# First block's attention: the weights' low halves by an accumulating DMA onto negated high halves, and every rotation on VectorE

## The reference, cut to what matters

```python
n = rmsnorm(h, attn_norm[l])
proj = n @ w_in[l]                                  # u, v_sgu, q, k, v_att: 512 columns each
...
q = apply_partial_rope(q, cos, sin)                 # 4 heads of 2 x 64; 16 of each 64 are rotated
k = apply_partial_rope(k, cos, sin)
... scores, causal softmax, p[:, :, 0] - lam * p[:, :, 1], times v_att ...
h = h + mixed @ w_out[l]                            # 512 rows from the gating, 512 from the attention
h = h + conv_ffn(rmsnorm(h, ffn_norm[l]), w_up[l], conv_w[l], conv_b[l], w_down[l])

def apply_partial_rope(t, cos, sin):
    half = ROT_DIM // 2
    t1 = t[..., :half]
    t2 = t[..., half:ROT_DIM]
    rot = jnp.concatenate([t1 * cos - t2 * sin, t2 * cos + t1 * sin], axis=-1)
    return jnp.concatenate([rot.astype(t.dtype), t[..., ROT_DIM:]], axis=-1)
```

## Time and profile before

| | |
|---|---|
| time, median of 3 runs (lowest to highest) | 1814.74 us (1811.52 to 1820.94) |
| the profiled execution: its time | 1814.2 us |
| its span in the profile | 1812.5 us |
| mean granted TensorE clock | 0.994 |

### The profile page before, as it was taken

How to read it: one execution, slowest core, us unless ns; L and a number is a source line. 1 busy time by engine, 2 the same in 40 slices (tenths; PEclk the granted TensorE clock), 3 DMA queues, 4 the chain that set the end, 5 groups by cost and what they waited for, 6 DMA issues and landing times. The chain is left out here.

```text
span 1812.5 us, 26067 instructions
## 1 busy us (share of the span) xinstructions
PE 1765.2 (97%) x8977; PEld 1440.3 (79%) x8977; DVE 1122.1 (62%) x1826; ACT 780.8 (43%) x1270; POOL 1037.3 (57%) x1265
## 2 busy tenths in 40 slices
PE   8999999999999999999999999999999999999998
PEld 6876888888888886788888888877666778988886
DVE  4788656566656338766666655644476567655665
ACT  5434543333334335453333333466566663333332
POOL 6574445555465557364555554457311558888885
PEclk9999999999999999999999999999999999999999
DMA  7221224443423221133444332413201112233221
GB/s 253 94 102 50 82 82 151 150 151 115 150 93 117 93 98 54 48 105 112 144 162 148 130 115 82 140 49 118 92 1 48 47 47 94 94 117 114 96 93 47
DMA packets 103206, 184.70 MB, mean 102 GB/s; under 512 B 7322, under 2 KB 67404, under 8 KB 101068
## 3 DMA queue, kind: packets, MB, share of 16 engines
q1 hardware_dynamic: 102940, 183.44, 28.8%
q10 hardware_dynamic: 176, 0.07, 0.0%
HBM read 180.35 MB, written 2.10 MB: 101 GB/s over the span
## 5 line engine op out<-in xcount | busy, mean ns | idle before, releaser
L1003 POOL TENSOR_TENSOR w_lo<-raw,w_hi 128x256 fp32r<-128x256 f32 (+1 forms) x1124 | 911.6, 845 | 751.0 <-ACT w_hi L1089 747.5
L2499 PE MATMUL ps<-n_hi,w_hi 128*128 128x512 f32 (+1 forms) x1320 | 507.1, 384 | 3.9 <-ACT zc L1394 1.8
L2501 PE MATMUL ps<-n_hi,w_lo 128*128 128x512 f32 (+1 forms) x1320 | 501.1, 380 | 0.0
L2500 PE MATMUL ps<-n_lo,w_hi 128*128 128x512 f32 (+1 forms) x1320 | 500.7, 379 | 0.0
L1089 ACT ACTIVATE w_hi<-raw 128x1024 fp32r<-128x1024 f32 (+2 forms) x331 | 307.8, 937 | 359.6 <-PE ps L2501 240.8
L2499 PEld LDWEIGHTS ps<-n_hi,w_hi 128*128 128x128 f32 x1320 | 249.0, 189 | 53.1 <-issue 6.0
L2501 PEld LDWEIGHTS ps<-n_hi,w_lo 128*128 128x128 f32 x1320 | 249.0, 189 | 48.0
L2500 PEld LDWEIGHTS ps<-n_lo,w_hi 128*128 128x128 f32 x1320 | 249.3, 189 | 45.4 <-issue 0.2
L2043 DVE TENSOR_TENSOR ps<-ps,sq 128x512 f32<-128x512 f32 x88 | 61.3, 699 | 179.8 <-PE ps L2501 177.4
L2499 PE MATMUL ps<-x_hi,w_hi 128*128 128x512 f32 x416 | 167.0, 401 | 0.1
L2501 PE MATMUL ps<-x_hi,w_lo 128*128 128x512 f32 x416 | 162.6, 391 | 0.0
(11 more groups left out here) (359 smaller groups left out, 2668.5 us busy)
## 6 DMA issues: line engine op xcount, KB each, us to landing
raw<-in_w_up SPq DMA_DIRECT2D x44, 1024.0 KB, 6.9
raw<-in_w_ff SPq DMA_DIRECT2D x32, 1024.0 KB, 6.6
raw<-in_w_in SPq DMA_DIRECT2D x26, 1024.0 KB, 6.1
zb<-in_ada_w SPq DMA_DIRECT2D x16, 1536.0 KB, 8.3
raw<-in_w_down SPq DMA_DIRECT2D x44, 512.0 KB, 3.9
raw<-in_w_out SPq DMA_DIRECT2D x12, 1024.0 KB, 6.1
raw<-in_w_in SPq DMA_DIRECT2D x4, 512.0 KB, 8.2
za<-in_x SPq DMA_DIRECT2D x4, 512.0 KB, 6.1
```

Source lines behind the costliest of these rows:

```text
L1003: last = pool.tensor_tensor(part[0], part[1], part[2], ALU.subtract)
L2499: pe.matmul(out, l_hi, r_hi, start=start, stop=False)
L2500: pe.matmul(out, l_hi, r_lo, start=False, stop=False)
L2501: return pe.matmul(out, l_lo, r_hi, start=False, stop=stop)
```

## The change

For the 32 quarters of the kinds `Q` and `D4` (16 in each layer) the low half is made in another way. ACT writes the high half as before and then, right behind it, the negated high half into `w_lo`. POOL, in place of four subtractions, waits for that, issues accumulating DMAs that add `raw` onto `w_lo` (four of 128x2x128 for a `Q` quarter, two of 128x2x256 for a `D4` one, two rows `k` each), waits until all have landed, and tells it with a small memset. Every rotation is on VectorE: heads 1 to 3, tile by tile, in the even steps 0 to 10 (`rope_at`). The waits of `swap_rows` are now for the DVE instruction that last read the half of `swapped`, two tiles back.

```diff
+ADDED_KINDS = ("Q", "D4")
+def rope_at(n):
+
+    return (1 + n // 4, n // 2 % 2) if n % 2 == 0 and n <= 10 else None
...
                     emptied(sp, ("qk"[j], l, t))
-                    if t == 0 and l:
-                        sp.wait_ge(rope_set, 6 * l - 1 + j)
-                    elif t == 1:
-                        sp.wait_ge(swap_read, 2 * l + 1 + j)
-                    elif t:
-                        sp.wait_ge(rope_set, 6 * l + 2 * t + j - 3)
+                    if n >= 2:
+                        sp.wait_ge(swap_read, n - 1)
...
+                if g in added_at:
+                    n = added_at[g]
+                    pool.wait_ge(wneg_ready, n + 1)
+                    to, raw_ = split_quarter(st.kind, w_lo.bitcast(F32), g % 4, q), source(st, q)
+                    for k in range(0, to.shape[1], 2):
+                        pool.dma_start(to[:, k:k + 2], raw_[:, k:k + 2], accum_op=ALU.add).then_inc(wadd_in, 16)
+                        added[0] += 16
+                    pool.wait_ge(wadd_in, added[0])
+                    pool.memset(mark[:, n % 8:n % 8 + 1], 0.0).then_inc(wlo_ready, 1)
+                    return
...
-            def rope(l, t, j):
-
-                x_ = (qT, kT)[j][:, t, :]
-                n = 8 * l + 2 * t + j
-                k = 2 * (6 * l + 2 * t + j - 2)
-                turned = swapped[:, n % 2, :]
-                if t == 1 and j == 0:
-                    pool.wait_ge(qk_ready, 2 * l + 2)
-                pool.wait_ge(swap_in[n % 2], 64 * (n // 2 + 1))
-                pool.tensor_tensor(x_, x_, cosF, ALU.mult).then_inc(rope_step, 1)
-                pool.tensor_tensor(turned, turned, sinF, ALU.mult).then_inc(rope_step, 1)
-                pool.wait_ge(rope_step, k + 2)
-                pool.tensor_tensor(x_, x_, turned, ALU.add).then_inc(rope_set, 1)
...
                 act.activation(split_quarter(st.kind, w_hi, g % 4, q), source(st, q),
                                ACT.Copy).then_inc(whi_ready, 1)
+                if g in added_at:
+                    act.activation(split_quarter(st.kind, w_lo, g % 4, q), source(st, q), ACT.Copy, scale=-1.0)\
+                        .then_inc(wneg_ready, 1)
...
                     x_ = (qT, kT)[j][:, t, :]
                     n = 8 * l + 2 * t + j
+                    if n >= 2:
+                        dve.wait_ge(qk_ready, n - 1)
                     dve.wait_ge(swap_in[n % 2], 64 * (n // 2 + 1))
...
-                    dve.wait_ge(swap_read, 2 * l + j + 1)
+                    dve.wait_ge(swap_read, n + 1)
...
+                    if (turned := rope_at(n)) is not None:
+                        rope(*turned)
                     if n < 2:
                         sgu_gate(2 + n)
```

More of the change, by code:

```diff
@@ L549, in build @@
         swapped = sb("swapped", [P, 2, S])
+        mark = sb("mark", [P, 8])
         banks = ctx.enter_context(nc.psum_tensor("ps", [P, 8 * S], F32))
@@ L557, in build @@
         whi_ready, wlo_ready = sem("whi_ready"), sem("wlo_ready")
+        wneg_ready, wadd_in = sem("wneg_ready"), sem("wadd_in")
         quarter_done = sem("quarter_done")
@@ L568, in build @@
         ang_ready, rope_ready = sem("ang_ready"), sem("rope_ready")
-        swap_zero, swap_read, rope_step, rope_set = (sem("swap_zero"), sem("swap_read"), sem("rope_step"),
-                                                     sem("rope_set"))
+        swap_zero, swap_read = sem("swap_zero"), sem("swap_read")
         swap_in = [sem(f"swap_in{i}") for i in range(2)]
@@ L739, in last_added @@
             return free[4 + i % 4], BK.ffn2[4 + i % 4] + 2 * (FG2 - 1) + i // 4 + 1
+        added_at = [st.at[q] for st, q in by_quarter if st.kind in ADDED_KINDS]
+        added_at = {g: n for n, g in enumerate(added_at)}
         def landed_value(st):
@@ L980, in _ @@
             pool.memset(swapped[:, :, :], 0.0).then_inc(swap_zero, 1)
+            added = [0]
             def lo(g, value, used, pieces=range(LO_PARTS)):
@@ L1026, in gains_and_weights @@
                 lo(g + 1, g + 2, g - 2, range(2, 4))
-            def rope(l, t, j):
-                x_ = (qT, kT)[j][:, t, :]
-                n = 8 * l + 2 * t + j
-                k = 2 * (6 * l + 2 * t + j - 2)
-                turned = swapped[:, n % 2, :]
-                if t == 1 and j == 0:
-                    pool.wait_ge(qk_ready, 2 * l + 2)
-                pool.wait_ge(swap_in[n % 2], 64 * (n // 2 + 1))
-                pool.tensor_tensor(x_, x_, cosF, ALU.mult).then_inc(rope_step, 1)
-                pool.tensor_tensor(turned, turned, sinF, ALU.mult).then_inc(rope_step, 1)
-                pool.wait_ge(rope_step, k + 2)
-                pool.tensor_tensor(x_, x_, turned, ALU.add).then_inc(rope_set, 1)
-            rope_before = {STR["qk", l, 0].g0 + 7 + i: (l, 1 + i // 2, i % 2) for l in range(DEPTH) for i in range(6)}
             done = 0
@@ L2744, in _ @@
                         if i == 0:
[L2745 to L2748, removed]
+                            pe.wait_ge(qk_ready, l * 8 + 2 * hd + 2)
                         for m in range(2):
```

2 lines of the change are left out of this document (removed).

## The result

The changed kernel takes 1961.96 us (median, 1956.12 to 1963.08) against 1814.75 of the kernel before. The ratio is 1.080, with a 95% interval of 1.0765 to 1.0836: slower by 147 us, far outside the predicted range.

What follows compares the result with a forecast made beforehand. PE, busy 97% of the span, was taken as the bound. Layer 0 +10.8, layer 1 -4.1, `D4` quarters +0.2 and DVE +1.4 made +8.3 us on 1814.2, 1822.5, hence 1823 against the median; range 1807 to 1852.

Steps and rivals of the forecast that it cites:

- What bounds: Whole kernel: PE is busy 97% of the span; the change could give back at most 13.5 us.
- which chain is hit: Layer 0, low half 15 to step 0's scores: scores may start at 98.7 + 3D, 118.8 against 108.60, +10.2 us.
- D: Time from a `Q` quarter's negated half being there to its `wlo_ready`: four issues, landing, memset; taken as 6.7 us.
- The price that decides: POOL's DMAs per `Q` quarter: between 4.0 and 10.2 us, taken as 6.7 with 1.12 per issue; 4.4 for `D4`.
- the signs of being wrong: In the changed profile: D outside 5.4 to 7.9, PE's longest new wait behind step 3, or L1975 staying at 0.66.
- Layer 1: Layer 1's attention: +1.1 at the scores, -3.5 values' wait, -3.4 and +1.7 clock; sum -4.1 us.
- the waits and the clock that I took as given back: Layer 1: the values' wait goes, -3.5 us, and the 0.87 clock stretch, -3.4; a new wait brings +1.7.
- The second rival: Head 2's swap behind `outa`'s load holds the softmax from step 4 if D > 7.6; +22 us at 8; chance 0.17.
- DVE's relief: DVE in the attention: without contention from POOL, 8 us come back per layer on L1975 and L1707; rotations then cost +0.7.
- ACT's cover: ACT's 32 instructions of 1.0 us lie in its idle time; without that cover they would cost 16 us a layer.
- The third rival: DVE becomes the bound in the attention: rotations cost +4 a layer, values' waits stay, +10 to +25 us; chance 0.07.
- The D4 quarters: Later quarters, two DMAs each: 4.4 us a quarter, what exceeds 4.3 is on the path, +0.1 us per layer.

Runs made afterwards that it cites:

- the copies: Changed kernel with POOL's DMAs copying `raw` onto `w_lo` instead of adding it (low parts wrong): 1838.63 against 1813.11 us, ratio 1.014.
- the long runs: Changed kernel with SP loading each quarter to its own contiguous 4 KB of a partition, added by one DMA of 128 runs: 1827.24 against 1813.44 us.

## Why the prediction was wrong

**What bounds, and which chain is hit: right.** The chain low half 15, load, swap, rotations, scores was put at 98.7 + 3D. With the copies, D = 6.5, that is 118.2, and the scores stood at 117.17. With the long runs, D = 4.7, it is 112.8, and they stood at 114.89. With D = 13.4 it is 138.9, and they stood at 142.68. The fit is closer than its parts, which is luck: from low half 15 to the scores I had 14.1 us, and it took 15.0, 17.6 and 15.4, while low half 15 itself came 1.9 and 1.4 us early in the first two and 2.5 late in the changed kernel, where quarter 12 was done only at 86.87 and not by 84.6.

**The price that decides: the step that failed.** I bounded D by 4.0 and 10.2 and took 6.7; it is 13.4, outside both ends. The issue's own price was good (1.21 us against 1.12). What failed was the thought that issues follow one another and land together. An added DMA of 256 runs leaves no room for a second, so four full rounds of issue and landing, 3.3 us each, stand one behind the other. My upper bound had this shape, but its round was 2.0 us, the landing of a plain store. The added 128 KB land 3.0 us after issue, and the next is issued 0.3 us later. The copied 128 KB land in 2.2 us, near the row that I used. For `D4` the same: two rounds, 7.7 us against 4.4. Two of the signs of being wrong that I had named came up: D is outside 5.4 to 7.9, and PE's longest new wait, 20.3 us, is behind step 3.

The Trainium skill (DMA: Bandwidth & Descriptors, section Anatomy of one DMA) gives 2.0 us plus bytes at 436 GB/s, an estimate of 2.3 us for 128 KB. For the copied one the trace agrees (2.2), for the added one it doesn't (3.0).

**Layer 1, and what lies beyond: a term left out.** With D = 6.5 my formulas gave about +7, and +25.5 was measured. A finished stripe lets SP's load go at the very time at which POOL issues the next quarter's DMAs, and these land behind 2 MB. In the kernel with copies, POOL in layer 1:

```profile
654.82 2.17 POOL L1001 DMA_DIRECT2D w_lo<-raw  x3
662.95 0.72 POOL L1001 DMA_DIRECT2D w_lo<-raw  x1 [5.96 <-issue]
```

and SP's queue there:

```profile
654.94 0.99 SPq L779 DMA_DIRECT2D raw<-in_w_in  x2
```

The pause is 5.96 us in place of 1.78, 4.2 more on the chain to step 0, and so the scores of layer 1 waited 6.2 us where I had +1.1 (at D = 6.7). The rest of the distance from +7 to +25.5 is in the waits and the clock that I took as given back and that were not (below), and in the last `D4` quarters. In the changed kernel the same thing costs 5.9 us at quarter 16 (7.95 against 2.10). The price per us of D is higher than mine, 7 up to D = 7.6 and 15 beyond: from 6.5 to 7.3 the time rose by some 15 us, and between 7.3 and 13.4 by 106, some 17 per us.

**The second rival, head 2's swap: the mechanism was right, and its threshold passed.** It was put at D > 7.6. The waits of 20.3 and 18.2 us are its mark, and moving the swap took them away and gave 23 us. The formula for it would have given some +105 at D = 13.4 (54 at 10, and 15 for each us more). Set against the table of matched matmuls, place by place: up to step 0 the formulas give 58 us in the two layers, 70 were measured; for head 2's swap 46, and the stretch that holds it added 51; for the last `D4` quarters 0.2, and 13 were measured. And 15 us lie between the scores of step 0 and of step 4, for which the sum has no term: PE waits there for quarters 16 and 17, 3.2 and 5.6 us in layer 0, because a quarter now takes over 13 us and its place in the softmax is two steps of 5.0. Collisions with loads have a part in these differences, and so have the slower matmuls, 32 us longer in all; how much each is was not taken apart.

**DVE's relief: right in cause; its value was not given back by the whole change.** L1975 fell from 662 to 160 ns as forecast. For the values' waits and the rotations together I had put -2.4 us in layer 0 and -2.8 in layer 1, besides 3.4 us of clock. With only the `D4` quarters by DMA the attention did gain 1.5 and 3.8 us, and lost more than that at the last of these quarters. With the long runs and head 0's swaps first it gained 2.7 us in layer 1 but lost 2.4 in layer 0: PE still waits 5.2 and 2.2 us for the values' product (3.1 and 3.5 before), and 2.4 and 2.1 for the turned ones (0.7 before). The rotations without relief were put at up to 4 us a layer and cost 2.9 and 0.7.

**ACT's cover: right,** 2.5 us of 33. **The third rival fell:** DVE is busy 21.3 of 61 us in the stretch where the loss arises, and POOL's issues took 1.20 to 1.22 us there, 1.21 in the median of the whole program.

**The D4 quarters: right in time by luck.** The +4.4 with only them by DMA holds 6.0 and 5.4 us of loss at the last one and about as much relief ahead of it. The term itself, +0.1 a layer, was wrong twice: the quarter takes 7.7 us and not 4.4, and the last one's first DMA is issued behind the load of `ada_w` and lands late.

How the rooms for runs are built no run tells. Shown are the counts, and that a pause ends 0.3 to 0.4 us after the last DMA issued before it has landed, while a landing without a pause does not start the count again. That there are two rooms, and what each is for, is argued from the counts. That the slower matmuls follow from the waits is argued too.

## What to carry to other kernels

Before a DMA from GpSimd replaces arithmetic, count its runs of contiguous memory, twice for one that adds, and see how many such DMAs can be issued in a row; if it is one, each costs its whole time to landing. Make the runs long by the layout of the load, then one DMA of 4 KB runs does in 4.7 us what four of 512 byte runs do in 13.4. Look at what the late result releases: here the load let go by it delayed the next small DMA from 3 to some 9 us, and with it all that stood behind that DMA in POOL's program. And when a part of a change costs nothing in the total, match the two traces instruction by instruction before calling it free: here a gain and a loss of 5 us a layer hid each other.

## What was not expected of the hardware

- Issues on GpSimd's DMA queue between pauses: 7 copied DMAs of 128 runs, 3 copied of 256, 1 added of 256. With added DMAs of 128 runs a pause stands behind every 3rd and every 7th, over all 192 of them, whether a run is 512 or 1024 bytes.
- Landing does not start that count again: it runs on over quarters at whose end POOL had waited until all was in.
- An added DMA is dearer than a copy in each part: issue 1.21 against 0.72 us, landing 3.0 against 2.2 us for 128 KB in 256 runs.
- 512 KB added in 128 runs of 4 KB: issue 0.86, landed 4.8 us after its issue in the median, against 13.4 us for 1024 runs in four DMAs.
- A DMA from GpSimd issued beside a 2 MB load landed 8.9 us after its issue (quarter 16, layer 0), against 3.0 in the median; all ten DMAs issued beside a large load took 7.2 to 11.0 us, and no other of the 96 over 4.5.
